# Gated layers of a two-block model: gated half of the output product inside the near units, and four changes of order elsewhere

## What is computed

```python
h = rmsnorm(x, mix_norm)
proj = h @ w_in          # na_q, na_k, na_v, g_q, g_k, g_v, g_r, gf_code, gb_code
na_o = rmsnorm(merge_heads(neighbourhood_attention(na_q, na_k, na_v, rpb)), na_gain)
log_gf = log_sigmoid(gf_code @ w_gate_f + b_gate_f) / GLA_TAU     # and log_gb
o_fwd, o_bwd = gla_chunked(g_q, g_k, g_v, log_gf, True), flip(gla_chunked(flip(...), log_gb, False))
gla_o = merge_heads(rmsnorm(o_fwd + o_bwd, gla_gain)) * silu(g_r)
x = x + concatenate([na_o, gla_o], axis=-1) @ w_out
```

## Time and profile before

| | |
|---|---|
| Median of 3 runs | 3377.82 us (3376.90 to 3381.84) |
| The profiled execution | 3382.92 us, span 3381.1 us |
| Granted TensorE clock, mean of its span | 0.982 of 2.4 GHz |
| PE busy | 3282.5 us, 97% |
| DVE, ACT, POOL busy | 1779.4, 1137.3, 403.4 us |
| Weights and other data moved | 293.19 MB, mean 87 GB/s |

### The profile page before, as it was taken

One profiled execution on the slowest core, in us unless ns is written; L12 is line 12 of the kernel. 1 busy time (PEld: TensorE's weight loads), 2 busy tenths in 40 slices (PEclk: granted clock), 3 DMA queues, 4 the chain that ended last, 5 costly groups with the idle time before them and its releaser, 6 DMA issues. The chain is left out here.

```text
span 3381.1 us, 40603 instructions
## 1 busy us (share of the span) xinstructions
PE 3282.5 (97%) x15310; PEld 2694.5 (80%) x15310; DVE 1779.4 (53%) x1907; ACT 1137.3 (34%) x1302; POOL 403.4 (12%) x319
## 2 busy tenths in 40 slices
PE   7999999999899999999999899999999999899998
PEld 5887888877688887888877788888888877788887
DVE  7774544459654455534574554345444575554444
ACT  3353222249432222322343333223322342423221
POOL 1001100110100024000252120002000242120002
PEclk9999999999999999999999899999999999899999
DMA  3111322232122224232211122324222211122222
GB/s 146 63 47 57 109 99 88 99 114 73 50 100 99 88 99 118 93 106 88 99 63 38 50 88 90 102 84 135 96 92 98 100 63 49 52 75 90 101 90 79
DMA packets 46196, 293.19 MB, mean 87 GB/s; under 512 B 5424, under 2 KB 5936, under 8 KB 17936
## 3 DMA queue, kind: packets, MB, share of 16 engines
q1 hardware_dynamic: 44640, 287.04, 24.3%
q0 software_dynamic: 1456, 4.79, 0.8%
HBM read 289.70 MB, written 2.10 MB: 86 GB/s over the span
## 5 line engine op out<-in xcount | busy, mean ns | idle before, releaser
L1779 DVE TENSOR_TENSOR w_lo<-w_raw,w_hi 128x2048 fp32r<-128x2048 f32 (+1 forms) x288 | 672.2, 2334 | 251.3 <-ACT w_hi L1391 251.2
L872 PE MATMUL ps<-xg_hi,w_hi 128*128 128x512 f32 x1920 | 749.6, 390 | 0.0
L872 PE MATMUL ps<-xg_hi,w_lo 128*128 128x512 f32 x1920 | 747.0, 389 | 0.0
L872 PE MATMUL ps<-xg_lo,w_hi 128*128 128x512 f32 x1920 | 747.0, 389 | 0.0
L1391 ACT ACTIVATE w_hi<-w_raw 128x2048 fp32r<-128x2048 f32 (+1 forms) x288 | 544.8, 1892 | 532.9 <-PE ps L872 357.7
L872 PE MATMUL ps<-hid_hi,w_hi 128*128 128x512 f32 x1216 | 473.4, 389 | 0.1
L872 PE MATMUL ps<-hid_hi,w_lo 128*128 128x512 f32 x1216 | 473.1, 389 | 0.0
L872 PE MATMUL ps<-hid_lo,w_hi 128*128 128x512 f32 x1216 | 473.0, 389 | 0.0
L872 PEld LDWEIGHTS ps<-xg_hi,w_hi 128*128 128x128 f32 x1920 | 360.6, 188 | 76.2 <-issue 1.7
L872 PEld LDWEIGHTS ps<-xg_lo,w_hi 128*128 128x128 f32 x1920 | 360.4, 188 | 76.3 <-issue 1.6
L872 PEld LDWEIGHTS ps<-xg_hi,w_lo 128*128 128x128 f32 x1920 | 360.4, 188 | 75.0
(11 more groups left out here) (360 smaller groups left out, 4092.4 us busy)
## 6 DMA issues: line engine op xcount, KB each, us to landing
w_raw<-up_dram SPq DMA_DIRECT2D x120, 1024.0 KB, 4.8
w_raw<-in_dram SPq DMA_DIRECT2D x42, 1024.0 KB, 4.8
w_raw<-down_dram SPq DMA_DIRECT2D x32, 1024.0 KB, 4.8
w_raw<-down_dram SPq DMA_DIRECT2D x32, 768.0 KB, 4.3
w_raw<-down_dram SPq DMA_DIRECT2D x32, 640.0 KB, 3.8
w_raw<-out_dram SPq DMA_DIRECT2D x14, 1024.0 KB, 4.8
w_raw<-out_dram SPq DMA_DIRECT2D x8, 768.0 KB, 4.4
w_raw<-memk_dram SPq DMA_DIRECT2D x4, 1024.0 KB, 4.9
```

What stands on the lines that cost most here:

```text
L872: last = pe.matmul(to, (w_hi, w_lo)[wp][:, q, t:t + P], parts[xp], start=(k == 0 and m == 0), stop=(k == p.ktiles - 1 and m == 2))
L1779: dve.tensor_tensor(w_lo[:, q, 0:w], w_raw[:, q, 0:w], w_hi[:, q, 0:w].bitcast(F32), ALU.subtract)\
```

## The change

1. **Gated layers.** The gate tiles come ahead of near queries and keys 2, 3, 6 and 7 and are kept in the free quarters of `nq` and `nk`; their silu and the product with `gfin` stand at units 0 and 1. All blocks are done by unit 1. The output weights are laid out anew: of the 4 slabs two hold the gated half of the rows for all 8 output tiles and two the near half. PE takes the gated half as eight pieces of 12 matmuls (`gated_out`), m = 0 to 5 in units 2 to 7 and 6 and 7 around the last `turn_out`; DVE adds each to x (`add`, L2422 of the new file). The near half is 8 pieces of 12 in 8 banks (`near_out`) behind it. The number of matmuls of the product stays 192.
2. **Softplus.** ACT does Abs, Exp and Ln in halves by direction, so that DVE's scans of the first can start earlier, and loads the function tables by one-element activations ahead of need.
3. **Start.** The first slab is split in two halves; of the rotary tables only the steps up to the turns stand ahead of the reciprocal, the remainders after the first slab's evictions.
4. **`out1_0` and middle norm.** The split of the next slab comes ahead of the epilogue on ACT and DVE; the middle norm's `token_rms` comes behind the whole first slab of its product instead of within it.
5. **Recurrent mixer's end.** The last `inward`, `front` of the first memory unit and `scores` of both memory units come earlier, and a slab's split moves from before the memory units into their second.

```diff
-                ph.append(Phase(f"out2_{l}", "resid", 4, 16, 2, src="mix", alpha=1.0, last=True, next_norm=norm + 1,
+                ph.append(Phase(f"out2_{l}", "resid", 4, 16, 4, src="mix", alpha=1.0, last=True, next_norm=norm + 1,
...
-GATED_TILES = (12, 13, 14, 15, 8, 9, 10, 11, 16, 17, 18, 19, 0, 1, 4, 5, 2, 3, 6, 7, 20, 21, 22, 23)
-NEAR_BLOCKS = ((14, 15), (16,), (17,), (18,), (19,), (), (), ())
+GATED_TILES = (12, 13, 14, 15, 8, 9, 10, 11, 16, 17, 18, 19, 0, 1, 4, 5, 20, 21, 22, 23, 2, 3, 6, 7)
+NEAR_BLOCKS = ((16, 17), (18, 19)) + ((),) * 6
+NEAR_OUT = ((), (), (0,), (1,), (2,), (3,), (4,), (5,))
...
-            if p.name in ("out2_0", "out2_1"):
-                second_out(p, src)
-                first = 1
             if rms is not None:
-                slab(0, 0, lambda: token_rms(rms))
+                if p.norm == MID + 1:
+                    slab(0, 0)
+                    token_rms(rms)
+                else:
+                    slab(0, 0, lambda: token_rms(rms))
...
+        def gated_out(l, m):
+            s, q, b = OUT2_AT[l] + m // 4, m // 4, m % 4
+            if m == 0:
+                pe.wait_ge(gy_ready, l + 1)
+            if b == 0:
+                pe.wait_ge(lo_done, s + 1)
+            if m < 2:
+                pe.wait_ge(evac, EV0 + Q * OUT2_AT[l])
+            else:
+                pe.wait_ge(evac, EV0 + Q * OUT2_AT[l] + m - 1)
+            for k in range(4):
+                t = (b * 4 + k) * P
+                for n, (wp, xp) in enumerate(TERMS):
+                    last = pe.matmul(ps[:, 6 + m % 2, :], (w_hi, w_lo)[wp][:, q, t:t + P], (mixG_hi, mixG_lo)[xp][:, k, :],
+                                     start=(k == 0 and n == 0), stop=(k == 3 and n == 2))
+            last.then_inc(mm_done, 1)
...
+        def near_out(p):
+            l, s0 = p.layer - 2, p.at["slab"] + 2
...
+            pe.wait_ge(ot_ready, SECTIONS[f"near{l}"][-1].f + 1)
+            for m in range(DT):
+                q, b = m // 4, m % 4
+                if b == 0:
+                    pe.wait_ge(lo_done, s0 + q + 1)
+                if m == 6:
...
+                last.then_inc(mm_done, 1)
...
+            block(13)
             turn_values(0)
             turn_values(1)
             scores(us[1])
-            block(13)
+            block(14)
             turn_values(2)
             turn_values(3)
+            block(15)
             pe.wait_ge(vt_ready, NVT[f"near{l}"] + NCB)
             for n, u in enumerate(us):
                 turn_probs(u)
                 if n + 2 == NCB:
-                    pe.wait_ge(evac, EV0 + Q * (s0 + 10))
+                    for m in NEAR_OUT[n]:
+                        gated_out(l, m)
+                    pe.wait_ge(evac, EV0 + Q * (s0 + 12))
                 if n + 2 < len(us):
                     scores(us[n + 2])
                 for t in NEAR_BLOCKS[n][:1]:
                     block(t)
+                if n + 2 != NCB:
+                    for m in NEAR_OUT[n]:
+                        gated_out(l, m)
                 if n and us[n - 1].last:
                     turn_out(us[n - 1])
                 weigh(u)
                 for t in NEAR_BLOCKS[n][1:]:
                     block(t)
+            gated_out(l, 6)
+            turn_out(us[-1])
+            gated_out(l, 7)
...
+            pe.wait_ge(gate_read, DT)
+            pe.wait_ge(evac, EV0 + Q * (MIX_O - 1))
+            scores(M1[0])
             pe.wait_ge(evac, EV0 + Q * MIX_O)
             for b in range(4):
                 out(0, 0, b)
-            pe.wait_ge(gate_read, DT)
-            scores(M1[0])
-            scores(M1[1])
+                if b == 2:
+                    scores(M1[1])
...
+                    ahead = p.name == "out1_0" and isinstance(i, int) and i == q == 0
+                    if ahead:
+                        split_high(s0 + 2, 0, p.tiles * P)
                     epilogue(i, q)
-                    if split:
+                    if split and not ahead:
...
+                if n + 1 == DT:
+                    gelu_square(n)
                 split(MIX_IN + n + 4)
                 if n + 1 < DT:
                     gates(n + 1, True)
                 else:
-                    gelu_square(n)
+                    exponentials(M1[0], 0)
...
-                act.wait_ge(gy_done, l + 1)
-                act.activation(gl[:], gy[:], ACT.Abs).then_inc(ga_done, 1)
-                act.wait_ge(ga_done, 2 * l + 1)
-                act.activation(gl[:], gl[:], ACT.Exp, scale=-1.0).then_inc(ga_done, 1)
-                act.wait_ge(ga_done, 2 * l + 2)
-                act.activation(gl[:], gl[:], ACT.Ln, bias=1.0).then_inc(gl_done, 1)
+                act.activation(warm[:], eps_c[:], ACT.Exp)
+                for d in range(2):
+                    act.wait_ge(gy_done, 2 * l + d + 1)
+                    act.activation(gl[:, d], gy[:, d], ACT.Abs).then_inc(ga_done, 1)
+                for d in range(2):
+                    act.wait_ge(ga_done, 4 * l + d + 1)
+                    act.activation(gl[:, d], gl[:, d], ACT.Exp, scale=-1.0).then_inc(ga_done, 1)
+                for d in range(2):
+                    act.wait_ge(ga_done, 4 * l + d + 3)
+                    act.activation(gl[:, d], gl[:, d], ACT.Ln, bias=1.0).then_inc(gl_done, 1)
...
+            act.activation(warm[:], eps_c[:], ACT.Exp)
...
-            for j in range(NCB):
-                turned_values(j)
+            turned_values(0)
+            turned_values(1)
+            split(10)
+            turned_values(2)
+            turned_values(3)
+            take_turned(us[0], 0)
+            act.wait_ge(evac, EV0 + Q * (s0 + 10))
+            for g in (nq, nk):
+                act.activation(g[:, 2:4, :], g[:, 2:4, :], ACT.Silu).then_inc(gsilu, 1)
+            exponentials(us[1], 1)
+            split(11)
             for n, u in enumerate(us):
+                if n == 0:
+                    continue
                 if n + 1 < len(us):
                     exponentials(us[n + 1], n + 1)
                 take_turned(u, n)
-                if n and us[n - 1].last:
+                if n == 1:
+                    act.wait_ge(g_out, 2 * (l + 1))
+                    act.activation(mixG_hi[:], gfin[:], ACT.Copy).then_inc(gy_hi, 1)
+                if us[n - 1].last:
                     square(us[n - 1])
-                if n in (0, 1):
-                    split(10 + n)
-                if n in (3, 5):
-                    split(12 + n // 5)
-                if n == 5:
-                    act.wait_ge(evac, EV0 + Q * (s0 + 12))
-                    act.activation(gate[:], gate[:], ACT.Silu).then_inc(gsilu, 1)
-                if n == 6:
-                    act.wait_ge(g_out, l + 1)
-                    act.activation(mixG_hi[:], gfin[:], ACT.Copy).then_inc(gy_hi, 1)
+                if n in (1, 2):
+                    split(11 + n)
+            split(14)
             square(us[-1])
+            split(15)
...
+                if p.name == "out1_0" and isinstance(i, int) and i == q == 0:
+                    split_low(s0 + 2, 0, p.tiles * P)
...
-                rope_tables(1)
+                rope_remainder(0)
+                rope_turns(1)
+                rope_remainder(1)
...
                     recur(n)
-                inward(n + 2)
-                split(MIX_IN + n + 4)
                 if n + 1 < DT:
+                    inward(n + 2)
+                    split(MIX_IN + n + 4)
                     inputs(n + 1)
+                else:
+                    front(M1[0], 0)
                 if n + 2 < DT:
                     conv(n + 2)
                 if n:
                     decays(n + 1)
                 else:
                     recur(n)
+                if n + 2 == DT:
+                    inward(DT + 1)
                 output(n)
+            split(MIX_O + 1)
             low(DT - 1)
-            split(MIX_O + 2)
-            front(M1[0], 0)
             front(M1[1], 1)
...
+                if n == 1:
+                    split(MIX_O + 2)
...
+                for n, g in enumerate((nq, nk)):
+                    h = slice(2 * n, 2 * n + 2)
+                    dve.wait_ge(gsilu, 2 * l + n + 1)
+                    dve.tensor_tensor(gfin[:, h, :], gfin[:, h, :], g[:, 2:4, :], ALU.mult).then_inc(g_out, 1)
...
+            block(13)
             front(us[1], 1)
-            block(13)
+            block(14)
+            split(10)
+            block(15)
             for n, u in enumerate(us):
+                if n + 2 == NCB:
+                    for m in NEAR_OUT[n]:
+                        add(m)
                 if n + 2 < len(us):
                     front(us[n + 2], n + 2)
                 if n and us[n - 1].last:
                     near_norm(us[n - 1])
-                if n in (2, 4, 6):
-                    split(10 + n // 2)
-                if n == 6:
+                if n == 0:
                     gate_out()
-                if n == 7:
-                    gate_low()
```

(23 more changed lines are left out.)

173 lines of the change are left out of this document (102 added, 71 removed).

## The result

The changed kernel takes **3328.61 us**, the median of four runs (3327.8 to 3329.5), against 3377.36 for the kernel before (3371.4 to 3381.8 in four runs). The ratio is 0.9853, with a 95% interval of 0.9841 to 0.9865: 48.8 us, or 1.5%, faster. The forecast was 3318 with a range of 3304 to 3343.

What follows compares the result with a forecast made beforehand. PE works 97% of the span, so only its idle and low-clock time can be won. Terms 9.5 + 4.7 + 9 + 4.5 + 8 + 24 = 59.7 off 3382.9 give 3323.2 profiled, 3318 median; own band 3308 to 3330, range 3304 to 3343.

Steps and rivals of the forecast that it cites:

- Start: Kernel start: first-eviction gap 5.9, clock 2.5 and half a split 1.1 us regained; −9.5, between −6 and −12.
- out1_0: At `out1_0`: wait of 3.3 us falls to 1.4 and 2.8 of clock is regained; −4.7, at least −1.9.
- mixer: Recurrent mixer's end: earlier `front` and `scores` remove waits and low clock; −9 us, between −5 and −11.
- middle norm: Middle norm: PE's 3.6 us wait for POOL's sums and 1.7 of clock go, 0.8 comes; −4.5, between −2 and −6.
- its +2.2: Recurrent mixer's end: cost in us of the slab's split moved into the second memory unit, ahead of a `finish`.
- Softplus: Both gated layers: wait of 4.8 us falls by 2.5, two thirds of lost clock returns; −8, between −3 and −11.
- Near part: Gated layers' near units and output product: 23.6 us of waits and clock less 9.8 and 1.0; −24 for two layers.
- POOL's lag: End of each gated layer: POOL's last sum of squares late by 1.0 us (0 to 3.5) at the next norm.
- this rule: DVE and POOL's shared port as exclusive lock: last two squares 3.21 us each, lag 4.2 a layer, gain 6.4 less.
- The second rival: Low clock stays at half of the places, where about 38 us of the gain hang on it; 3337, chance 0.15.
- The unit chain: Near units: DVE, ACT and POOL keep the 9.25 us pace, so 9 us a layer less gain; 3336, chance 0.13.
- the slower case: Gated layers: alternating wide and narrow matmuls drop PE to 1.2 GHz from unit 2; net +68, 3446, chance 0.04.

Runs made afterwards that it cites:

- experiments 3 and 7: Kernel before with twelve useless matmuls ahead of `turn_out` in units 5 to 7, 3369.78 us; the same with DVE's gate product cut to one column, 3368.10 us.
- experiments 4 and 5: Changed kernel with ACT squaring the last two tiles, 3323.49 us; changed kernel with DVE's first output slab split ahead of the last block's eviction, 3323.46 us.
- Experiment 4: Changed kernel with ACT squaring the last two tiles of x after each gated layer's output product, POOL only adding them; 3323.49 us.
- The first and second experiment: Changed kernel with gated near part and output product in the old order, 3349.95 us; kernel before with the new near part and output product alone, 3361.37 us.
- experiment 8: Changed kernel with the softplus in halves but without its early table loads; 3337.32 us, ratio to before 0.9882.

## Why the prediction was right, and where its steps were off

The measured time lies in the range and in the forecast's own band, and the mechanism was right: gaps closed and clock regained at the places named. The forecast promised 10.6 us more than came, though, by the steps below.

**Start, `out1_0`, mixer, middle norm.** Predicted 9.5, 4.7, 9 and 4.5, measured 9.0, 4.9, 8.6 and 4.6. The waits came as worked out: 0.2 and 0.4 at the start, 1.0 at `out1_0` (1.4 was expected), 2.4 ahead of `finish` in the mixer, which was its +2.2. That the clock came back with the waits was right in all four windows. But the dips that it was counted from are not in every run: in experiments 3 and 7 `out1_0` is as before, with the same wait of 3.31 us, and has no dip behind it. So that 2.8 of the 4.7 were there to be regained was luck of the profile. The wait of 2.4 in the mixer is over the 2 us that the prediction set as its sign there, though its own sum had it. What the step on the start had not seen is the reason for the long angle steps of the earlier trace rows: they were POOL's doing, and the new order leaves a race that some runs lose (the profiles of experiments 4 and 5).

**Softplus.** Predicted 8, of which 5 were waits and 3 clock; measured 6.4. Mis-sized were the waits above all: they fell from 4.77 to 2.66 in the second layer and to 1.72 + 1.30 in the first, where the second wait, for the copy of the bank, had not been listed; 3.9 in place of 5.0. The remaining 2.5 is the clock, which in the second head is 0.85 still.

**Near part.** Predicted 24, measured 21.2, and the sum hides two errors. The units gave more: the waits that were listed at 9.8 us a layer are 7.1 in the profile (2.2, 0.2, 1.1, 0.4, 0.4, 1.2 and 1.6), and up to the near output a layer is 14.9 us shorter where 13.8 was worked out. The step that failed is POOL's lag: it was put at 1.0 us a layer, between 0 and 3.5, and is 4.15, a wait of 2.63 and 1.5 lost to a half-clock stretch behind it. Two sizes were wrong in it. The prediction read 1.61 us as POOL's sum beside a free DVE, where it is 1.28, and it let the 3.21 in only as the far end of its range. Its sign, POOL's last square within 1 us of PE's end of the near output, failed: that square begins 3.7 us behind it (1939.19 against 1935.5). POOL (and DVE's splits below it) in the changed kernel:

```profile
1929.83 1.29 POOL L685 TENSOR_TENSOR ssq<-ssq,sq 128x512 f32<-128x512 f32 x1
1931.30 1.27 POOL L683 TENSOR_TENSOR sq<-x 128x512 f32 x1 [0.18 <-POOL ssq L685]
1932.64 3.21 POOL L685 TENSOR_TENSOR ssq<-ssq,sq 128x512 f32<-128x512 f32 x1
1936.03 1.27 POOL L683 TENSOR_TENSOR sq<-x 128x512 f32 x1 [0.18 <-POOL ssq L685]
1937.38 1.63 POOL L685 TENSOR_TENSOR ssq<-ssq,sq 128x512 f32<-128x512 f32 x1
1939.19 1.27 POOL L683 TENSOR_TENSOR sq<-x 128x512 f32 x1 [0.18 <-POOL ssq L685]
1940.54 3.19 POOL L685 TENSOR_TENSOR ssq<-ssq,sq 128x512 f32<-128x512 f32 x1
...
1931.59 3.12 DVE L1840 TENSOR_TENSOR w_lo<-w_raw,w_hi 128x2048 fp32r<-128x2048 f32 x1
...
1939.61 3.00 DVE L1840 TENSOR_TENSOR w_lo<-w_raw,w_hi 128x2048 fp32r<-128x2048 f32 x1
```

A square and its sum take 1.27 + 1.28 us and 0.3 between them, 2.8 a tile, as long as PE's 12 matmuls (2.76): POOL cannot catch up once it is late. Two of its sums take 3.2 us: each begins inside a split of DVE and ends 1.1 us behind that split's end (1934.71, 1942.61). The splits take 3.12 and 3.00 in place of 2.28, as each began while a square was running. In the old order 24 matmuls of PE stood against the same 2.8, and the one collision of the earlier trace rows was absorbed. Experiment 4 shows that the lag is the cause: the wait and the dip go together when two squares are taken off POOL.

The rows fit an exclusive lock, not a sharing of speed: the sum that had 2.07 us beside the split still needed 1.14 of its 1.28 us behind it. This is what the Trainium skill (SBUF — State Buffer, SBUF: two separate sides) states of the port pair that DVE and GpSimd share: whichever instruction starts first gets it for its whole length. The prediction had set this rule beside the row's 1.0 with 4.2 us a layer, and with it the sum would have been 53.3, not 59.7, against 54.8 measured. The two collisions a layer bear out the rule. That 4.2 meets 4.15 is luck in part: the rule's 4.2 was all wait, with the last two tiles colliding, and measured were a wait of 2.63 and a dip, with the sixth and the eighth.

**From the profile to the median.** The prediction took the 5.1 us between the profiled execution of before and its median off again, for both kernels. After, profile and median agree within 0.6. So the median fell 48.8 us and not 54.8: the profiled run of before was one of its longest (3382.9 in a range of 3371 to 3383), with the long start and with dips that other runs lack. Of the 10.6 us between forecast and result 4.9 are terms of the sum and 5.7 this step.

**Rivals.** The second rival's sum was added wrongly: its terms make 35.8 and not 38, which moves its 3337 by 1. The unit chain does not set the pace at 9.25: it is 6.45 in the changed kernel, with DVE idle for 1.87 us in each unit. The low clock did not stay. The first and second experiment show that the near part and the rest each pay. The clock did not fall under the alternation of wide and narrow matmuls: 1.00 over units 5 to 7, so nothing here bore out the rule cited for the slower case (the Trainium skill, TensorE: Matmul & The Clock Gate, A second HAM failure mode: psum-queue depth-cycling).

What remains open is when a wait is followed by a dip. The 13 profiles together show that its length alone does not decide. No wait of 1.5 to 1.8 us had one; 2.23 us ahead of the first piece had one in 3 of 14 cases, 2.37 in the mixer in 3 of 8, 2.27 in the attention (165 to 174 us) in 13 of 13, 2.63 to 2.65 at the norms in 14 of 14, 3.31 at `out1_0` in 2 of 4. And some dips stand where PE had not waited, at 1796 and 2810 us in the changed kernel. No run was made for that.

## What to carry to other kernels

When a filler closes a wait on the critical engine, list what ran in that wait's shadow on every other engine: here POOL's squares had twice the time that they need per tile before and just that time after, and that one line was worth 8 us. Work used as filler should be work that has to be done anyway; useless matmuls bought back waits and clock but charged for themselves. A dip of the clock in one profile is not yet a gain: look whether it stands in other runs of the same code before it is counted. And before a median is forecast from one profile, look whether that profile is a typical run: a race of 0.3 us between two engines moved the whole profile by 3.4 us.

## What the runs showed of the hardware that was not expected

- A DVE instruction with SBUF operands (`tensor_scalar` of 512 columns, 0.43 us) took 3.71 us when it began 0.37 us behind a POOL instruction of 3.79, while DVE's reciprocal of 512 columns (3.35 us) ran through one of 3.6 us without delay, and evictions of 512 columns from PSUM (0.69, 1.29 for two) were not longer beside POOL in any of the profiles.
- It works both ways: POOL's sum of 1.28 us took 3.2 when it began inside a DVE split (2.28 alone).
- Half clock follows some waits of 2.2 us and not others of the same length (3 of 14 at one place, 13 of 13 at another), 3.31 us at `out1_0` had none behind it in two of four profiles, and dips worth 1.5 us come and go far from an edit (experiment 8).
